# A two-block transformer kernel: other buffers, issue orders and last step in its MLP

## The chip, the cores and the metric

One core of a Trainium2 chip runs the whole program. The metric is the device time of one execution in microseconds, the median of several. Every number below is of this kernel on this chip.

## The reference

Two transformer blocks over 1024 rows of 1024 float32 values; the first (two layers of windowed attention and mLSTM) and the second's mixers are not touched. The change lies in the second block's last lines:

```python
x = x + y @ w_out[l]
xn2 = _rmsnorm(x, norm2_g[l])
x = x + jnp.square(jax.nn.relu(xn2 @ w_up[l])) @ w_down[l]   # 1024 -> 4096 -> 1024
return _rmsnorm(x, final_g)
```

## The kernel before

**Precision.** Float32 factors are split in two parts, a rounded high part (written by ScalarE, `*_hi`) and the rest (`*_lo`, a subtraction by VectorE, DVE, or by GpSimd, POOL). A product is three matmuls: high by high, high by low, low by high. DVE's subtraction is called a split here.

**Seven products.** Both MLP matrices are multiplied by a scheme of seven block products (numbers 1 to 7) in place of eight. Each factor is cut in four blocks; sums of blocks (s1 to s4 of the up weights, t1 to t4 of the down weights, hs1 to hs4 of the hidden part, and row sums of the normed input) are formed by POOL and DVE; the products are added up in seven shared sums.

**Output product and norm** (`output`). TensorE (PE) makes 16 products of 24 matmuls, eight row tiles for each of two column halves. In the second half each tile is added to `x_res` (`residual`), squared (ScalarE), scaled (DVE, `scale_rows`, after POOL's `root`), turned by PE (`turn`, eight transposes), split (`low_rows` for tiles 0 to 3) and, for tiles 4 to 7, made into the row sums that products 5, 6, 7, 3 and 4 need (`rows_low` on DVE: seven instructions; `rows_high` on ScalarE; `low_third` on POOL). The sum for number 4 is made once, by DVE and POOL, and its split is in `up(0)`.

**Up phase** (`up`). Sixteen groups g of 256 hidden units, seven products of 12 matmuls each, in the order `UP_ORDER` = 1, 5, 2, 6, 7, 3, 4. For each group SP's queue loads one 1 MB piece of raw weights (`u_raw`), after all seven splits of the group before; POOL makes s1 to s4 (`sums_up`); ScalarE rounds, DVE splits (`low_up(g + 1, j)`, placed late in `up(g)`), DVE adds PSUM results to h11, u_two, u_four, h22, h21, h12 and squares the four h; POOL makes hs1 to hs4 (`sums_hidden`); SP stores h11, h12, h22 (`store_hidden`) and the sums (`store_sums`) to DRAM. DVE's first addition of a group (h11) waits for the sums and the store of the last group, since they share one buffer.

**Down phase** (`down`). Eight steps w of 512 hidden units, each seven products j of four tiles of 6 matmuls, in the order `DN_ORDER`. SP loads the hidden parts (`load_hidden(w, j)`, each into the slot that product j of the step before frees) and the weights (`load_down`, two halves of `d_raw`). POOL makes t1 to t4 and five of the low parts (`LOW_POOL`); DVE makes the other nine (`LOW_DVE`, by position) and 28 additions. Tile i of the down phase writes bank (i + 4) % 8 and waits until tile i - 8's bank was read (`q_add`); the first eight wait for the up phase's additions. In the last step the shared sums are joined, and then `finish` adds the last four tiles, and each row is squared, scaled and stored from one of two buffers.

**What sets the order.** Each engine runs its instructions in the order of the program; semaphores join them. SP's queue is one such order too: a load behind a wait stands.

## Time and profile before

| | us |
|---|---|
| median of 3 runs | 2792.64 (2783.29 to 2793.39) |
| the profiled execution | 2788.39 |
| its span, first to last instruction | 2786.6 |
| PE busy | 2614.4 (94%) |
| DVE busy | 1758.1 (63%) |
| POOL busy | 861.1 (31%) |
| mean granted TensorE clock | 0.973 |

The profile is of one execution. The changed phases take about its last quarter: output product from 2003, up phase from 2096, down phase from 2437, end at 2786.6. Matmuls are pipelined, so the pitch from start to start tells the pace of PE, and the idle time before an instruction, in brackets, tells what it waited for.

### The profile page before, as it was taken

Reading aid. Unit: us, or ns where it says so; the run is one execution under the profiler, and the core shown is the slowest. Engines: PE = TensorE matmul, PEld = TensorE weight load, DVE = VectorE, ACT = ScalarE, POOL = GpSimd, SP = SyncE. Lnnn points to the kernel's source line nnn. Section 1 sums busy time; section 2 is a strip of 40 time slices with the busy share of each in tenths; the row PEclk is TensorE's granted clock in tenths of the full one; section 3 lists DMA queues with packets and bytes.
Section 4 is the critical chain, followed back from the end, with each engine's and each line's share of the span. In section 5 each row is a group of like instructions: output and inputs, shape, how many; then the busy total and the mean of one; then the engine's idle time right before and its main releaser. Section 6 shows DMA issues by size and latency. Waiting matters only on the chain. (4 is left out here: it accounts for less than half of the span.)

```text
span 2786.6 us, 37933 instructions
## 1 busy us (share of the span) xinstructions
PE 2614.4 (94%) x14936; PEld 2159.8 (78%) x14936; DVE 1758.1 (63%) x2677; ACT 1058.1 (38%) x1999; POOL 861.1 (31%) x582
## 2 busy tenths in 40 slices
PE   6999999999998999999989989999998999889995
PEld 4789888888866798888878768856686877668884
DVE  4312575676544413766765546868648787789998
ACT  3201233666522311335656334278613222233332
POOL 0000100234531001101326400046104656577665
PEclk8999999999999999999999999999999999999998
DMA  7322222136565222321264421100301434454441
GB/s 281 97 87 82 80 76 80 38 92 213 181 233 208 96 77 71 99 80 49 63 216 158 167 98 47 40 16 1 144 1 57 158 134 163 166 184 152 145 159 68
DMA packets 182255, 317.23 MB, mean 114 GB/s; under 512 B 29138, under 2 KB 110724, under 8 KB 174016
## 3 DMA queue, kind: packets, MB, share of 16 engines
q1 hardware_dynamic: 160928, 300.08, 31.9%
q10 hardware_dynamic: 21152, 14.75, 1.7%
q8 instruction: 119, 1.95, 0.3%
q14 instruction: 56, 0.46, 0.1%
HBM read 237.04 MB, written 72.50 MB: 111 GB/s over the span
## 5 line engine op out<-in xcount | busy, mean ns | idle before, releaser
L1026 PE MATMUL ps<-xn_hi_sb,ft_hi_sb 128*128 128x512 f32 (+1 forms) x720 | 264.0, 367 | 1.0 <-DVE ft_lo_sb L1477 1.0
L1027 PE MATMUL ps<-xn_lo_sb,ft_hi_sb 128*128 128x512 f32 (+1 forms) x720 | 263.2, 366 | 0.0
L1028 PE MATMUL ps<-xn_hi_sb,ft_lo_sb 128*128 128x512 f32 (+1 forms) x720 | 262.9, 365 | 0.0
L978 PE MATMUL ps<-tm_hi_sb,xn_hi_sb 128*128 128x512 f32 (+2 forms) x608 | 216.0, 355 | 14.8 <-DVE xn_lo_sb L1391 6.7
L980 PE MATMUL ps<-tm_hi_sb,xn_lo_sb 128*128 128x512 f32 (+2 forms) x608 | 213.3, 351 | 0.0
L979 PE MATMUL ps<-tm_lo_sb,xn_hi_sb 128*128 128x512 f32 (+2 forms) x608 | 213.1, 350 | 0.0
L2285 POOL TENSOR_TENSOR arena_sb<-arena_sb 128x1024 f32<-128x1024 f32 x10 | 25.9, 2591 | 418.7 <-ACT arena_sb L2000 418.7
L1026 PEld LDWEIGHTS ps<-xn_hi_sb,ft_hi_sb 128*128 128x128 f32 x720 | 136.8, 190 | 23.4 <-DVE ft_lo_sb L1477 1.4
L1027 PEld LDWEIGHTS ps<-xn_lo_sb,ft_hi_sb 128*128 128x128 f32 x720 | 136.9, 190 | 21.6
L1028 PEld LDWEIGHTS ps<-xn_hi_sb,ft_lo_sb 128*128 128x128 f32 x720 | 136.8, 190 | 21.7
L2081 ACT ACTIVATE arena_sb<-ps,neg_max_sb 128x640 f32<-128x640 f32 (+1 forms) x144 | 109.3, 759 | 103.7 <-DVE neg_max_sb L1644 97.7
L1643 DVE TENSOR_REDUCE row_max_sb<-ps 128x1 f32<-128x640 f32 (+1 forms) x144 | 111.7, 776 | 46.9 <-PE ps L1073 46.0
L978 PEld LDWEIGHTS ps<-tm_hi_sb,xn_hi_sb 128*128 128x128 f32 x608 | 115.1, 189 | 33.5 <-issue 9.3
L3845 POOL TENSOR_TENSOR arena_sb<-arena_sb 128x512 f32<-128x512 f32 x60 | 75.2, 1274 | 188.0 <-DVE arena_sb L3164 188.0
L2305 POOL CAST q_hl_sb<-arena_sb 64x512 fp32r<-64x512 f32 x36 | 24.2, 671 | 327.9 <-PE ps L1028 289.9
L980 PEld LDWEIGHTS ps<-tm_hi_sb,xn_lo_sb 128*128 128x128 f32 x608 | 115.0, 189 | 11.9
L979 PEld LDWEIGHTS ps<-tm_lo_sb,xn_hi_sb 128*128 128x128 f32 x608 | 115.3, 190 | 10.9
L1083 PE MATMUL ps<-ident_sb,arena_sb 128*128 128x128 f32 x672 | 107.7, 287 | 15.9 <-ACT arena_sb L2081 10.3
L2993 PE MATMUL ps<-xn_hi_sb 128*128 128x512 f32 x256 | 101.2, 395 | 11.2 <-DVE xn_lo_sb L3393 8.2
L2955 PE MATMUL ps<-xn_hi_sb,uq_hi_sb 128*128 128x512 f32 x256 | 102.0, 399 | 10.1 <-DVE uq_lo_sb L3267 6.0
L1226 PE MATMUL ps<-w_out_hi_sb,mix_hi_sb 128*128 128x512 f32 x256 | 105.8, 413 | 4.5 <-DVE mix_lo_sb L1830 4.5
L2272 POOL TENSOR_TENSOR stat_sb<-stat_sb,minus_half_sb 128x1 f32<-128x1 f32 (+1 forms) x48 | 35.7, 743 | 236.2 <-DVE stat_sb L1356 128.4
(491 smaller groups left out, 7505.4 us busy)
## 6 DMA issues: line engine op xcount, KB each, us to landing
arena_sb<-in_w_ft SPq DMA_DIRECT2D x44, 512.0 KB, 3.3
arena_sb<-mqk_dram SPq DMA_DIRECT2D x36, 512.0 KB, 3.7
arena_sb<-x_dram SPq DMA_DIRECT2D x33, 512.0 KB, 7.0
arena_sb<-in_w_ada SPq DMA_DIRECT2D x16, 1024.0 KB, 9.0
u_raw_sb<-in_w_up SPq DMA_DIRECT2D x16, 1024.0 KB, 4.9
hq_dram<-h_part_sb SPq DMA_DIRECT2D x16, 1024.0 KB, 4.1
d_raw_sb<-in_w_down SPq DMA_DIRECT2D x16, 1024.0 KB, 5.6
xn_raw_sb<-hq_dram SPq DMA_DIRECT2D x32, 512.0 KB, 3.6
```

The source lines that it names most:

```text
L978: pe.matmul(at, hi, tm_hi[b][:, k, :], start=k == 0, stop=False)
L979: pe.matmul(at, hi, tm_lo[b][:, k, :], start=False, stop=False)
L980: mm = pe.matmul(at, lo, tm_hi[b][:, k, :], start=False, stop=k == KT - 1)
L1026: pe.matmul(to, hi, xn_hi_flat[:, k, at:at + size], start=k == 0, stop=False)
L1027: pe.matmul(to, hi, xn_lo_flat[:, k, at:at + size], start=False, stop=False)
L1028: mm = pe.matmul(to, lo, xn_hi_flat[:, k, at:at + size], start=False, stop=k == KT - 1)
L1083: mm = pe.transpose(ps[:, bank, at * P:(at + 1) * P], prob[h % 2][:, n * P:(n + 1) * P], ident[:, :])
L1226: pe.matmul(to, hi, w_hi, start=start, stop=False)
L1643: ch(dve, dve.tensor_reduce(row_max[:, u, h:h + 1], at, AX_X, ALU.max, negate=True))
L2081: act.activation(prob[r][:, 0:n], at, ACT.Exp, bias=neg_max[:, u, h:h + 1], scale=DH ** -0.5, accum_out=lsum[:, u, h:h + 1]).then_inc(a_e[ ...
L2955: pe.matmul(to, uq_hi[n][:, k, :], xq_hi[n][:, k, :], start=k == 0, stop=False)
L2993: pe.matmul(to, aq_hi[j][:, k, rows], bq_hi[j][:, k, :], start=k == 0, stop=False)
```

## The change

In the up phase the raw weights get another layout in DRAM. Three of the four blocks stay in one buffer (`u_raw`), the fourth (u22) has two; s3 and s4 get raw buffers of their own. A load waits for the first three splits and the sums of the group before, and for the fourth block for the splits two groups back; it stands ahead of `store_hidden` on SP. DVE's splits are spread over the group, the first at its head. The stored pair is now h11 and h22.

In `output` the row sums of tiles 4 to 7 are two instructions before the scaling of the next tile, one between its mean and its scaling, two behind; ScalarE makes copies for them (`first_high`, and in `rows_high`). The turn of tile 6 comes before the first up product. DVE adds the sum for number 4 instead of POOL.

`DN_ORDER` becomes 1, 2, 6, 5, 3, 7, 4. The splits for down step 0 stand between the additions of up group 15. In steps 0 to 5, DVE makes the splits of positions 5 and 6 ahead of the last four additions. The last step (512 units) is eight plain block products in place of seven: 16 output tiles of 12 matmuls, row by row; groups 14 and 15 need no hidden sums, and POOL makes only two low parts. DVE joins the shared sums for rows 0 to 3, POOL for rows 4 to 7, and each row is squared, scaled and stored as it ends.

```diff
 xq_hi[n], xq_lo[n] = rounded(f"xq{n}_hi", at, 4, HALF), rounded(f"xq{n}_lo", at + 2048, 4, HALF)
...
-u_raw = apart("u_raw", M2, KT, FG)
-u11, u12, u21, u22 = [u_raw[:, 4 * k:4 * k + 4, P * n:P * n + P] for n in range(2) for k in range(2)]
-u_at = [M2 + 2048 + 1024 * j for j in range(6)] + [M2 + 17984]
+u_raw = apart("u_raw", M2, 3, 4, P)
+u11, u12, u21 = [u_raw[:, n] for n in range(3)]
+u22 = [apart(f"u22{i}", at, 4, P) for i, at in enumerate((M2 + 1536, M2 + 16448))]
...
-LOW_DVE = ((0, 0), (0, 1), (2, 0), (2, 1), (3, 1), (1, 1), (4, 1), (5, 1), (6, 1))
-LOW_POOL = (3, 1, 4, 5, 6)
+LAST = WIDE - 1
+LOW_DVE = ((0, 0), (0, 1), (1, 0), (1, 1), (2, 1), (3, 1), (4, 1), (5, 1), (6, 1))
...
+def raw_free(g):
+    if g > 0:
+        sp.wait_ge(u_lo, 7 * g - 4)
+        sp.wait_ge(u_sum, 4 * g)
 def load_up(g):
-    sp.dma_start(u_raw, A["w_up"][g]).then_inc(u_ld, 16)
+    raw_free(g)
+    sp.dma_start(u_raw, A["w_up"][g][:, 0:3]).then_inc(u_ld, 16)
+    if g == 1:
+        sp.wait_ge(norm_sems["2"]["tr"], NX - 1)
+    elif g > 1:
+        sp.wait_ge(u_lo, 7 * g - 7)
+    sp.dma_start(u22[g % 2], A["w_up"][g][:, 3]).then_inc(u_ld, 16)
...
+    sp.wait_ge(u_h, 4 * g + 2)
+    sp.dma_start(hq_dram[g // 2][:, 0:2, g % 2, :], h_part[:, 0:2, :]).then_inc(hq_a, 16)
 def store_sums(g):
+    if g // 2 == LAST:
+        sp.wait_ge(u_h, 4 * g + 4)
+        sp.dma_start(hq_dram[LAST][:, 5:7, g % 2, :], h_part[:, 5:8:2, :]).then_inc(hq_s, 16)
...
-for g in range(GROUPS):
-    if g + 1 < GROUPS:
-        sp.wait_ge(u_lo, 7 * g + 7)
-        load_up(g + 1)
+load_up(1)
+for g in range(GROUPS - 1):
     if g > 0:
         store_sums(g - 1)
-    if g + 1 < GROUPS:
-        store_hidden(g)
-sp.wait_ge(u_lo, 7 * GROUPS)
-load_down(0, 0)
+    if g + 2 < GROUPS:
+        load_up(g + 2)
+    else:
+        raw_free(GROUPS)
+        sp.wait_ge(u_lo, 7 * GROUPS - 7)
+        load_down(0, 0)
+    store_hidden(g)
+store_sums(GROUPS - 2)
 load_hidden(0, 0)
 sp.wait_ge(up_mm, up_no(GROUPS - 1, 5))
 load_down(0, 1)
...
     load_hidden(0, j)
 store_hidden(GROUPS - 1)
+for j in range(5, 7):
+    load_hidden(0, j)
...
-    load_hidden(w, 0)
     sp.wait_ge(t_sum, 4 * w - 1)
     sp.wait_ge(q_lo, 9 * w - 7)
     load_down(w, 0)
+    load_hidden(w, 0)
     sp.wait_ge(t_sum, 4 * w)
-    sp.wait_ge(q_lo, 9 * w - 1)
+    sp.wait_ge(q_lo, 9 * w - 2)
     load_down(w, 1)
-    for j in range(1, 7):
+    for j in range(1, 4 if w == LAST else 7):
...
     pe.wait_ge(norm_sems["2"]["ev_dve"], 4)
     product(0, 1)
-    turn("2", nx_s2, NX - 2, 0)
+    turn("2", nx_s2, NX - 1, 1)
     product(0, 2)
-    turn("2", nx_s2, NX - 1, 1)
...
+    def last_product(t, c):
+        i, row, rows = 28 * LAST + 2 * t + c, t // 4, slice(t % 4 * P, (t % 4 + 1) * P)
+        if t % 4 == 0:
+            pe.wait_ge(q_lo, 9 * LAST + 6)
+            pe.wait_ge(q_lop, 5 * LAST + 2)
+        to = ps[:, (i + 4) % 8, :]
+        pe.wait_ge(q_add, i - 7)
+        for m in range(2):
+            a, b = 2 * row + m, 2 * c + m
+            for k in range(2):
+                pe.matmul(to, aq_hi[a][:, k, rows], bq_hi[b][:, k, :], start=m == 0 and k == 0, stop=False)
+                pe.matmul(to, aq_hi[a][:, k, rows], bq_lo[b][:, k, :], start=False, stop=False)
+                mm = pe.matmul(to, aq_lo[a][:, k, rows], bq_hi[b][:, k, :], start=False, stop=m == 1 and k == 1)
+        mm.then_inc(q_mm2, 1)
+    for w in range(LAST):
...
+    def first_rows(t):
+        t1 = xq_raw[5][:, :, at]
         dve.wait_ge(s["tr"], t + 1)
+        dve.tensor_tensor(t1, top, t1, ALU.subtract).then_inc(t_row, 1)
+        dve.wait_ge(t_high, high_t(n, "x22"))
+        dve.tensor_tensor(xq_lo[3][:, :, at], bottom, xq_hi[3][:, :, at].bitcast(F32), ALU.subtract).then_inc(t_row, 1)
+    def second_rows(t):
+        u, n, at = t % 2, t - 4, slice((t - 4) * P, (t - 3) * P)
+        bottom = ps[:, 2 * u + 1, :].rearrange("p (k q) -> p k q", k=4)
+        dve.wait_ge(t_row, row_no(n, "t1"))
+        dve.tensor_tensor(xq_raw[6][:, :, at], bottom, xq_raw[5][:, :, at], ALU.subtract).then_inc(t_row, 1)
+    def third_rows(t):
+        s, u, n, at = norm_sems["2"], t % 2, t - 4, slice((t - 4) * P, (t - 3) * P)
+        bottom = ps[:, 2 * u + 1, :].rearrange("p (k q) -> p k q", k=4)
+        t3 = xq_raw[7][:, :, at]
         dve.wait_ge(s["ev_act"], t + 1)
+        dve.tensor_tensor(t3, bottom, t3, ALU.subtract).then_inc(s["ev_dve"], 1)
         dve.wait_ge(t_high, high_t(n, "t1"))
+        dve.wait_ge(t_row, row_no(n, "t2"))
+        dve.tensor_tensor(xq_lo[5][:, :, at], xq_raw[5][:, :, at], xq_hi[5][:, :, at].bitcast(F32), ALU.subtract).then_inc(t_low, 1)
...
     dve.wait_ge(g2_ld, 16)
     for t in range(NX):
         residual(1, t)
-        scale_rows("2", x_res[:, t, :], g2_row, nx_s2[t % 2], t)
         if 1 <= t <= 4:
             low_rows("2", xn2_hi, xn2_lo, t - 1)
         elif t > 4:
-            rows_low(t - 1)
-    rows_low(NX - 1)
+            first_rows(t - 1)
+        mean_square("2", t)
+        if t > 4:
+            second_rows(t - 1)
+        scale_row("2", x_res[:, t, :], g2_row, nx_s2[t % 2], t)
+        if t > 4:
...
+        lows(0)
+        dve.wait_ge(hq_a, 16 * g)
+        dve.wait_ge(u_hs, min(4 * g - 1, 4 * (GROUPS - 2)))
     dve.wait_ge(up_mm, up_no(g, 2))
     dve.wait_ge(u_p1, g + 1)
-    if g > 0:
-        dve.wait_ge(hq_a, 16 * g)
-        dve.wait_ge(u_hs, 4 * g)
     dve.tensor_tensor(h11, p1_copy, bank(2), ALU.add).then_inc(u_add, 1)
+    if g == 0:
+        lows(0)
+        dve.wait_ge(t_high, 17)
+        dve.tensor_tensor(xq_lo[4], xq_raw[4], xq_hi[4].bitcast(F32), ALU.subtract).then_inc(t_low, 1)
+    lows(1)
     dve.wait_ge(up_mm, up_no(g, 6))
     dve.tensor_tensor(u_two, p1_copy, bank(6), ALU.add).then_inc(u_add, 1)
     dve.wait_ge(u_add, add_no(g, "c11"))
     squared(h11).then_inc(u_h, 1)
-    if g == 0:
-        dve.wait_ge(t_high, 13)
-        dve.tensor_tensor(xq_lo[4], xq_raw[4], xq_hi[4].bitcast(F32), ALU.subtract).then_inc(t_low, 1)
     dve.wait_ge(up_mm, up_no(g, 5))
     dve.wait_ge(u_add, add_no(g, "u2"))
     dve.tensor_tensor(u_four, u_two, bank(5), ALU.add).then_inc(u_add, 1)
-    if g + 1 < GROUPS:
-        low_up(g + 1, 0)
-        low_up(g + 1, 1)
-        low_up(g + 1, 2)
+    lows(2)
+    next_quads(0, 1)
     dve.wait_ge(up_mm, up_no(g, 7))
     dve.wait_ge(u_add, add_no(g, "u4"))
     dve.tensor_tensor(h22, u_four, bank(7), ALU.add).then_inc(u_add, 1)
     dve.tensor_tensor(u_two, u_two, bank(7), ALU.add).then_inc(u_add, 1)
-    dve.wait_ge(up_mm, up_no(g, 3))
-    dve.tensor_tensor(h21, u_four, bank(3), ALU.add).then_inc(u_add, 1)
+    lows(3)
     dve.wait_ge(u_add, add_no(g, "c22"))
     squared(h22).then_inc(u_h, 1)
+    lows(4)
+    next_quads(2, 3)
+    dve.wait_ge(up_mm, up_no(g, 3))
+    if g == GROUPS - 1:
+        dve.wait_ge(hq_s, 16 * g)
+    dve.tensor_tensor(h21, u_four, bank(3), ALU.add).then_inc(u_add, 1)
     dve.wait_ge(u_add, add_no(g, "c12"))
     squared(h21).then_inc(u_h, 1)
-    if g + 1 < GROUPS:
-        low_up(g + 1, 3)
-        low_up(g + 1, 4)
-    else:
-        for m in range(4):
-            low_quad(0, *LOW_DVE[m])
+    lows(5)
+    next_quads(4, 5)
     dve.wait_ge(up_mm, up_no(g, 4))
     dve.wait_ge(u_add, add_no(g, "u7"))
+    if 0 < g < GROUPS - 1:
+        dve.wait_ge(hq_s, 16 * g)
     dve.tensor_tensor(h12, u_two, bank(4), ALU.add).then_inc(u_add, 1)
     dve.wait_ge(u_add, add_no(g, "c21"))
     squared(h12).then_inc(u_h, 1)
-    if g + 1 < GROUPS:
-        low_up(g + 1, 5)
-        low_up(g + 1, 6)
-    else:
-        for m in range(4, 7):
-            low_quad(0, *LOW_DVE[m])
+    lows(6)
+    next_quads(6)
 def low_quad(w, j, b):
...
+    def lows(*which):
+        for m in which:
+            if w + 1 < LAST or m < 6:
+                low_quad(w + 1, *LOW_DVE[m])
...
-        join(lambda t: sum6[t], sum1)
-    for t in range(4):
...
+def last_down():
...
+    def add(t, c):
+        i = 28 * LAST + 2 * t + c
+        x = x_res[:, t, 512 * c:512 * (c + 1)]
+        dve.wait_ge(q_mm2, i + 1)
+        dve.wait_ge(q_both, 8 + 2 * t + c + 1) if t < 4 else dve.wait_ge(q_join, 4 * (t - 4) + 2 * (c + 1))
+        dve.tensor_tensor(x, x, ps[:, (i + 4) % 8, :], ALU.add).then_inc(q_add, 1)
...
-    pool.tensor_tensor(s1, u21, u22, ALU.add).then_inc(u_sum, 1)
+    pool.tensor_tensor(s1, u21, u22[g % 2], ALU.add).then_inc(u_sum, 1)
+    if g == 1:
+        pool.wait_ge(norm_sems["2"]["tr"], NX)
+    if g > 0:
+        pool.wait_ge(u_lo, 7 * g - 2)
+    pool.tensor_tensor(s3_raw, u11, u21, ALU.subtract).then_inc(u_sum, 1)
     if g > 0:
         pool.wait_ge(up_mm, up_no(g - 1, 6))
     pool.wait_ge(u_sum, 4 * g + 1)
     pool.tensor_tensor(s2, s1, u11, ALU.subtract).then_inc(u_sum, 1)
-    if g > 0:
-        pool.wait_ge(up_mm, up_no(g - 1, 3))
-    pool.wait_ge(u_sum, 4 * g + 2)
-    pool.tensor_tensor(s4, u12, s2, ALU.subtract).then_inc(u_sum, 1)
+        pool.wait_ge(u_lo, 7 * g - 1)
+    pool.wait_ge(u_sum, 4 * g + 3)
...
+    if w == LAST:
+        low_quad(2)
+        low_quad(3)
...
+    low_quad(2)
     low_quad(3)
-    low_quad(1)
-    if w == 0:
-        sums_hidden(GROUPS - 1)
-    slot_free(pool, w, 4)
+    slot_free(pool, w, 5)
     pool.tensor_tensor(t3, b22, b12, ALU.subtract).then_inc(t_sum, 1)
     low_quad(4)
-    low_quad(5)
     slot_free(pool, w, 6)
     pool.wait_ge(t_sum, 4 * w + 2)
     pool.tensor_tensor(t4, b21, t2_raw, ALU.subtract).then_inc(t_sum, 1)
+    low_quad(5)
     low_quad(6)
+def last_joins(t):
+    for c, what in ((0, sum6), (0, sum7), (1, sum5), (1, sum7)):
+        x = x_res[:, 4 + t, 512 * c:512 * (c + 1)]
+        if what is sum7:
+            pool.wait_ge(q_join, 4 * t + 2 * c + 1)
+        pool.tensor_tensor(x, x, what[t], ALU.add).then_inc(q_join, 1)
 sums_up(0)
```

## Rows read from the trace of the kernel before

**Rows 1.** Busy time by stretch; the first line names the columns.
```profile
core 0: us, PE busy (x) PEld busy (x) DVE busy (x) ACT busy (x) POOL busy (x), PEclk, DMA share, GB/s
2096.00:2134.00 38.00, 26.64 (x103) 20.77 (x102) 33.40 (x35) 13.04 (x20) 16.50 (x8) 0.82 0.08 28
2134.00:2429.00 295.00, 288.93 (x1260) 235.19 (x1259) 231.21 (x272) 67.92 (x116) 178.33 (x118) 1.00 0.39 144
2429.00:2463.00 34.00, 16.44 (x54) 12.41 (x53) 19.51 (x17) 12.64 (x13) 26.21 (x12) 0.77 0.73 273
2463.00:2719.00 256.00, 256.00 (x1126) 211.27 (x1125) 253.57 (x250) 96.20 (x96) 176.93 (x62) 1.00 0.45 152
2757.00:2787.00 30.00, 0.20 (x1) 0.00 (x0) 20.78 (x32) 8.97 (x16) 6.91 (x9) 0.57 0.34 140
```
**Rows 2.** Waits, 2134 to 2429 (who <- for whom: total us, times, longest).
```profile
ACT uq_hi_sb L3523 <- DMA u_raw_sb<-in_w_up: 162.9, 14, 11.9
...
DVE h_part_sb L3341 <- POOL h_part_sb L3882: 58.4, 15, 3.9
```
**Rows 3.** Timeline of PE: starts of two up groups, of two down steps.
```profile
2153.12 0.50 PE L2955 MATMUL ps<-xn_hi_sb,uq_hi_sb 128*128 128x512 f32 x1
...
2172.79 0.50 PE L2955 MATMUL ps<-xn_hi_sb,uq_hi_sb 128*128 128x512 f32 x1 [0.34 <-DVE uq_lo_sb L3267]
...
2566.64 0.39 PE L2993 MATMUL ps<-xn_hi_sb 128*128 128x512 f32 x1
...
2604.72 0.39 PE L2993 MATMUL ps<-xn_hi_sb 128*128 128x512 f32 x1
```
**Rows 4.** Up group 0: line L2955 (durations, first and last start), timelines.
```profile
L2955 PE MATMUL ps<-xn_hi_sb,uq_hi_sb x256: 389/389/792, 2096.1 to 2425.8; 128*128 128x512 f32 x128
...
2103.58 2.27 DVE L3040 SCALAR_TENSOR_TENSOR arena_sb<-arena_sb,stat_sb,small_sb 128x1024 f32<-128x1024 f32 x1 [0.66 <-POOL stat_sb L3825]
...
2111.86 0.79 PE L2955 MATMUL ps<-xn_hi_sb,uq_hi_sb 128*128 128x512 f32 x1 [3.98 <-DVE xn_lo_sb L3286]
...
2118.11 6.67 POOL L3929 TENSOR_TENSOR xq_raw_sb<-xq_raw_sb,xn_lo_sb 128x2048 f32<-128x2048 f32 x1
...
2124.81 1.92 ACT L3775 ACTIVATE xq_hi_sb<-xq_raw_sb 128x2048 fp32r<-128x2048 f32 x1 [9.43 <-POOL xq_raw_sb L3929]
...
2129.38 0.50 PE L2955 MATMUL ps<-xq_hi_sb,uq_hi_sb 128*128 128x512 f32 x1 [3.25 <-DVE xq_lo_sb L3348]
...
2133.83 0.39 PE L2955 MATMUL ps<-xn_hi_sb,uq_hi_sb 128*128 128x512 f32 x1
```
**Rows 5.** Timelines of DVE and POOL inside one down step.
```profile
2580.46 1.21 DVE L3393 TENSOR_TENSOR xq_lo_sb<-xq_raw_sb,xq_hi_sb 128x1024 fp32r<-128x1024 f32 x1
...
2594.42 5.76 POOL L3896 TENSOR_TENSOR xq_lo_sb<-xq_raw_sb,xq_hi_sb 128x1024 fp32r<-128x1024 f32 x2
...
2597.86 3.41 DVE L3393 TENSOR_TENSOR xq_lo_sb<-xq_raw_sb,xq_hi_sb 128x1024 fp32r<-128x1024 f32 x1
...
2606.91 2.47 DVE L3409 TENSOR_TENSOR arena_sb<-arena_sb,ps 128x512 f32<-128x512 f32 x4
```
**Rows 6.** Timelines of SP's queue and PE at the hand-over.
```profile
2425.35 0.50 SPq L2612 DMA_DIRECT2D d_raw_sb<-in_w_down  x1
...
2428.98 0.39 PE L2957 MATMUL ps<-xq_hi_sb,uq_lo_sb 128*128 128x512 f32 x1
...
2461.17 0.77 PE L2993 MATMUL ps<-xn_hi_sb 128*128 128x512 f32 x1 [3.04 <-DVE sum_sb L3407]
```
**Rows 7.** Timelines of the last down step and the tail.
```profile
2718.96 0.39 PE L2993 MATMUL ps<-xn_hi_sb 128*128 128x512 f32 x1
...
2756.82 0.39 PE L2995 MATMUL ps<-xq_hi_sb,xq_lo_sb 128*128 128x512 f32 x1
...
2773.80 1.06 ACT L3511 ACTIVATE arena_sb<-arena_sb 128x1024 f32<-128x1024 f32 x1 [0.75 <-DVE stat_sb L3019]
...
2776.06 0.54 POOL L3825 TENSOR_TENSOR stat_sb<-stat_sb,minus_half_sb 128x1 f32<-128x1 f32 x1 [1.76 <-DVE stat_sb L3019]
...
2780.64 1.28 DVE L3326 SCALAR_TENSOR_TENSOR out_s_sb<-arena_sb,stat_sb,final_g_sb 128x1024 f32<-128x1024 f32 x1 [0.56 <-DMA out<-out_s_sb]
```

268 lines of the change are left out of this document (128 added, 140 removed).

## The prediction

> **What bounds the kernel now.** I read the busy time by stage first, then what waited for whom, then the timelines around each gap. TensorE sets the time. From the first product of the up phase to the last of the down phase it issues matmuls back to back except in four places [rows 1]. The pitch: product 0 of one down step starts at 2566.64 and of the next at 2604.72 [rows 3]; 168 matmuls lie between, so 38.08/168 = 0.2267 us each, a product of 12 matmuls takes 2.72 us, and an up group of 84 takes 19.04 us. What is over that is the loss. (a) Up group 0 starts at 2096.1, group 1 at 2133.83 [rows 4]: 37.7 where 19.0 would do, loss 18.7. (b) Groups 1 to 15 end at 2429.2 (last matmul plus one pitch [rows 6]): 295.4 where 15 x 19.04 = 285.6 would do, loss 9.8; in the row of one boundary the groups start 19.67 apart [rows 3]. (c) The third product of the down phase starts at 2461.17, where 2429.2 + 4 x 2.72 = 2440.1 was possible, and its first matmuls still last 0.77 [rows 6]: loss 21 and about 1.5 of slow clock, 22.5. (d) After the last matmul (2756.82) comes a tail up to 2786.6: 29.8 [rows 7].
>
> Two waits explain (b): the loads of raw weights, on which ScalarE waits 162.9 us in all, and DVE's first addition of a group, which waits 58.4 us for POOL's sums of the hidden part [rows 2]. The splits then come in a burst and the next group's first one is late.
>
> **Part 1, raw weights in two buffers, loads first in SP's order.** The load of group g+2 now goes when the third split of g+1 and POOL's four sums are done, and the first split of the next group stands at the head of DVE's group. I walked one group (its first product starts at 0). POOL's s2 waits for the product of number 6 (10.9) and ends near 12.4 (1.2, half of POOL's 2.3 at 1024 wide [rows 5]). DVE's operations from there are short: 0.6 each for additions out of PSUM (2.47 for four [rows 5]) and, at half the width of the 1.21 split, 0.6 for a split or a square; twelve or so bring it to 23. DVE next has to be at h11 at 8.5 of the following group, which is 27.5. The store of h11 goes at 19.1 behind the load on SP and has 8 us to land; the load goes at 16.8 and is needed at 22. All have over 3 us to spare, so (b) goes: -9.5. What is late next is nothing within 3 us. Behind the new wait of SP (third split of g+1) stands the store of h11, and behind that DVE's h11; if the cover of 4 us were gone, each microsecond would cost 15.
>
> **Part 2, row norm interleaved.** The row sums of one tile go from seven DVE instructions to five, and the scaled row stands between them, not before them. Before, DVE delayed the scaled row of the last tile to 2103.58 and product three of group 0 to 2111.86 [rows 4]. In the new order DVE's tile costs seven operations of 0.6 or so (additions out of PSUM, below), the scaling at 1.2 (1.28 with its overlap [rows 7]), in all near 5 us, under TensorE's 24 matmuls and one turn a tile (24 x 0.2267 = 5.4 and the turn); 1.1 more where POOL's third split collides with the scaling (2.27 instead of 1.28 [rows 4, 7]). I get: scaled row 6 at 2096.3, scaled row 7 at 2103.8, the turn until 2104.8, product three at 2104.9. So 7 us earlier; but TensorE still idles 3.6 before that turn, and runs slow again for some 2 us, as after the gap of 3.25, where 12 matmuls took 2133.83 - 2129.38 = 4.45 instead of 2.72 [rows 4]. The sum for number 4 leaves POOL (6.67 beside DVE [rows 4]) for DVE (2.3). It is followed by ScalarE's rounding (1.92 [rows 4]), a first split of group 1 that waits for its rounding, and the 2048-wide split (2.3, twice the 1.13 of a 1024-wide one): ready near 2123, while TensorE asks at 2120.5; with the product and a slow start group 1 begins at 2127.3. Gain 6.5; 5 to 9 are open.
>
> **Part 3, hand-over to the down phase.** Before, the down weights went out at 2425.35, behind the store of the sums [rows 6], and groups 14 and 15 had sums to store. Now d_raw's first half goes in group 14, hidden part 0 goes at 4 us of group 15, and DVE's splits stand between its additions. With free engines product 0 would be ready at 15, before TensorE asks (19.05), and (c) would vanish. But POOL's 2.3 us operations and DVE's with two SBUF inputs do not overlap: alone DVE's split takes 1.21, beside POOL 3.41, and POOL's pair takes 5.76 [rows 5]. The order is strictly alternating in these rows: 3.41 is POOL's 2.3 and then DVE's 1.1. In group 15 POOL has nine such operations from 11.2 on (product 6 frees t1's slot) and DVE seven splits and four squares, each of which waits for one of POOL's. Step by step: t1 to 13.4, square 14.0, t2 16.3, split 17.4, POOL 19.7, split 20.8: product 0 starts at 21 (late 2.0). Then POOL 23.1, square 23.7, POOL 26, split 27.1, POOL 29.4, split 30.5: product 1 starts at 30.6 instead of 26.4 (4.2). Then h21, square behind POOL 33.4, split 36.8, split 40.2, and h12 only at 40.8: the eighth down tile needs the bank that h12 reads and stands from 34.8 to 40.9 (6.1, in which the slow clock after the earlier gap is hidden); 0.6 more for the ninth tile, and 1.5 of slow clock. Loss 14.4 instead of 22.5: gain 8. Ends: nothing gained, if loads land 8 us late as several did in 2429 to 2463 (DMA share 0.73 [rows 1]); 22.5 if POOL's operations come in other gaps.
>
> The Trainium skill (SBUF — State Buffer, section Who interferes with whom) says that a DVE instruction with two SBUF inputs and a GpSimd instruction that reads SBUF exclude each other for their whole length, and that the issue order decides who waits. The rows at 3.41 against 1.21 agree; if they shared bandwidth evenly instead, the alternation above would not hold and this part would be worth more.
>
> **Part 4, down steps.** Products have another order, and DVE now makes two splits (positions 5 and 6 of LOW_DVE) ahead of the last four additions of a step instead of one. In the profile these additions begin at 2606.91 [rows 5]; one more split beside POOL is +3.40, the first addition ends at 2610.31 + 0.60 = 2610.9. The bank it frees is wanted by tile 5 of the next step at 2604.72 + 5.44 = 2610.16. So TensorE waits 0.8 in each of six steps: +5 (0 to 8; at 0 if POOL's ops end a little earlier). The clock stays high over such gaps, as over the 0.34 at a group boundary [rows 3]; I take that to hold for 0.8 too.
>
> **Part 5, the last 512 units by plain products.** 16 tiles of 12 matmuls instead of 168: +24 x 0.2267 = +5.4. Against it the tail shrinks, since tiles finish row by row. Before, from the first matmul of the last step (2718.96) to the end is 67.7 [rows 7]. After: TensorE ends at 43.5. DVE's 16 joins start at 1 and collide with POOL's four to a row; DVE is at its first addition at 15.8, loses 1.1 to POOL's joins at each scaling, and waits for root 3, which stands behind POOL's fourth row of joins (37.5). It catches up at 2.5 us a row: additions of row 7 at 45.0, square 1.25 and root 0.54 [rows 7], last scaling ends at 48.3. From the last scaling's end (2780.64 + 1.28) to the end of the span were 4.7, so 53.0. Gain 14.7, against 17 if DVE were never late and 10 if POOL's joins cost 5 us more.
>
> **Sum.** 9.5 + 6.5 + 8 - 5 + 14.5 = 33.5. The profiled execution took 2788.4 (span 2786.6), so 2755; it lies 4.2 under the median of the runs shown (2792.6), and against that median the sum gives 2759. I take 2758, since the runs spread over 10 us.
>
> **Rivals.** *A: the hand-over and the down steps keep TensorE fed* (POOL's operations fall beside additions out of PSUM, which don't collide). For: in the profile 256 us of the down phase pass without a gap though DVE is shown busy all the time [rows 1]. Against: the alternation in [rows 5]. Gain 9.5 + 6.5 + 22 + 0 + 14.5 = 52: 2740. *B: the hand-over only moves its wait and the last step is bound by POOL's 16 joins*: 9.5 + 4 + 0 - 7 + 9 = 15: 2777. *C, slower: the chain SP to DVE in the up phase.* The store of h11 stands on SP behind a load that waits for the third split of the next group, h11 of the next group waits for that store, and the splits come behind h11. If that ring takes longer than a group's 19.04, every group is late. It has about 4 us of slack by my walk; it decides from there, and to eat 48 us (33.5 and 14 more) it has to run at 22.3 a group: 2807. Against it: DVE is busy 231 of 295 [rows 1] and POOL 178, waiting for each other included. *D: the change doesn't remove the boundary waits* (a split of the next group is still last): 24 of gain, 2769, inside my range.
>
> **How the numbers follow.** Chances: forecast with its neighbours (D too) 0.68, A 0.15, B 0.11, C 0.06. Range 2742 to 2775: it takes in the bounds of part 3 and part 4 up to nearly A and nearly B. A measurement of this kernel can tell about 0.5% (14 us) from no change. B is half under that, so faster 0.87, same 0.08, slower 0.05.
>
> **What would show it.** Up groups 19.05 apart with no gap before their first matmul (part 1); product three of group 0 near 2105 and group 1 near 2127; down product 1 waiting for DVE's split and the eighth down tile waiting for h12 (part 3); gaps of 0.8 before the fifth tile of each down step, released by DVE's addition (part 4); a tail after the last matmul near 9.5 us instead of 29.8. Wrong would be: groups over 19.5 apart, or a hand-over with loads as its last wait.

## The result, and the profile after

| | before | changed |
|---|---|---|
| median, us | 2788.62 (4 runs, 2783.29 to 2793.39) | 2757.02 (4 runs, 2754.36 to 2764.34) |
| the profiled execution | 2788.39 | 2755.82 |
| its span | 2786.6 | 2754.1 |
| mean granted TensorE clock | 0.973 | 0.979 |

The ratio is 0.9891 with a 95% interval of 0.9861 to 0.9921: 1.1% faster. The forecast was 2758, from 2742 to 2775. The median before now has a fourth run in it (2784.6); the prediction reckoned from 2792.64, the median of the first three.

First the windows of the changed kernel's profile, cut at its own stage bounds, in answer to [rows 1] (time, then busy us and count for PE, weight loads, DVE, ACT and POOL, granted clock, DMA share, GB/s):

```profile
2097.00:2126.00 29.00, 22.53 (x97) 17.94 (x96) 25.90 (x26) 13.24 (x21) 12.34 (x8) 0.94 0.03 10
2126.00:2413.00 287.00, 287.00 (x1261) 236.36 (x1259) 214.45 (x270) 75.75 (x122) 177.06 (x115) 1.00 0.45 162
2413.00:2437.00 24.00, 14.72 (x50) 10.73 (x49) 23.93 (x15) 6.46 (x7) 19.70 (x7) 0.83 0.23 81
2437.00:2700.00 263.00, 258.66 (x1130) 212.28 (x1130) 252.48 (x256) 92.34 (x92) 161.06 (x56) 1.00 0.46 151
2743.00:2754.00 11.00, 0.56 (x3) 0.13 (x1) 5.59 (x8) 2.30 (x4) 1.55 (x3) 0.65 0.47 191
```

PE is now busy for all of the 287 us of groups 1 to 15. What is left lies in up group 0 (22.5 busy of 29), in the hand-over (14.7 of 24) and, new, in the down steps: 258.7 of 263, where the kernel before was busy for all of 256. To put numbers on it I take from the timelines the start of each stage's first matmul, and call "loss" what a stage takes over its matmuls times 0.2267 us.

| stage | before | changed | difference | forecast |
|---|---|---|---|---|
| start of the execution to the output product | 2003.25 | 2002.02 | -1.2 (same code) | 0 |
| output product to group 1's start | 130.58 | 123.99 | -6.6 | -6.5 |
| groups 1 to 15, loss | 9.78 | 1.60 | -8.2 | -9.5 |
| end of up phase to down product 2, loss | 21.09 | 13.08 | -8.0 | -8 |
| product 2 to the last step, loss | 2.07 | 6.99 | +4.9 | +5 |
| last step and tail | 67.65 | 54.18 | -13.5 | -14.5 |
| sum | | | -32.6 | -33.5 |

Two rows of this table share a boundary that the forecast drew elsewhere. In the kernel before, 1.6 us of slow matmuls follow the start of down product 2 (granted clock 0.50 from 2461.2 to 2464.0), in the changed kernel 1.0; the forecast counted them in the hand-over, the table in the row below. By the forecast's cut the hand-over gained 8.6 (for 8) and the down steps cost 5.5 (for 5).

The loads no longer stand in the way. Waits between 2126 and 2413, in answer to [rows 2] (who waits for whom: total us, times, longest); 162.9 us of waiting have become 3.2:

```profile
DVE h_part_sb L3411 <- PE ps L2983: 20.2, 12, 4.8
...
ACT uq_hi_sb L3578 <- DMA u_sb<-in_w_up: 3.2, 4, 1.4
```

PE's timeline, in answer to [rows 3] (start, duration, engine, line, operation; in brackets idle time before it and what ended it). Two groups start 19.14 apart with no bracket, two down steps 39.09 apart where it was 38.08, and inside the step stands a wait for DVE's addition:

```profile
2126.01 0.39 PE L2981 MATMUL ps<-xn_hi_sb,uq_hi_sb 128*128 128x512 f32 x1
...
2145.15 0.39 PE L2981 MATMUL ps<-xn_hi_sb,uq_hi_sb 128*128 128x512 f32 x1
...
2465.35 0.39 PE L3018 MATMUL ps<-xn_hi_sb 128*128 128x512 f32 x1
...
2471.68 0.47 PE L3018 MATMUL ps<-xq_hi_sb 128*128 128x512 f32 x1 [0.73 <-DVE arena_sb L3479]
...
2504.44 0.39 PE L3018 MATMUL ps<-xn_hi_sb 128*128 128x512 f32 x1
```

Group 0, all engines, in answer to [rows 4]. The last scaling now ends at 2103.57, product number 2 of the group starts behind the turn at 2104.48, and product number 4 waits for its split (L3415):

```profile
2101.29 2.28 DVE L3087 SCALAR_TENSOR_TENSOR arena_sb<-arena_sb,stat_sb,small_sb 128x1024 f32<-128x1024 f32 x1
...
2103.63 1.09 PE L2693 MATMUL ps<-ident_sb,arena_sb 128*128 128x128 f32 x8 [3.33 <-DVE arena_sb L3087]
2104.48 0.60 PE L2981 MATMUL ps<-xn_hi_sb,uq_hi_sb 128*128 128x512 f32 x1
...
2118.07 1.71 DVE L3314 TENSOR_TENSOR uq_lo_sb<-u_raw_sb,uq_hi_sb 128x512 fp32r<-128x512 f32 x1 [1.91 <-ACT uq_hi_sb L3578]
2119.70 3.35 DVE L3415 TENSOR_TENSOR xq_lo_sb<-xq_raw_sb,xq_hi_sb 128x2048 fp32r<-128x2048 f32 x1
...
2123.11 0.50 PE L2981 MATMUL ps<-xq_hi_sb,uq_hi_sb 128*128 128x512 f32 x1 [3.13 <-DVE xq_lo_sb L3415]
```

The hand-over, in answer to [rows 6]. The down weights go out at 2391.01, 22 us ahead of the end of the up phase, where it was 4 (2425.35 and 2429.2). PE now waits three times, always for DVE, and of DVE's seven splits there five take 3.4 us (the first 2.85; the last, with GpSimd done, 1.22). DVE has no idle time between 2405.2 and 2436, so it wasn't waiting for a load or for ScalarE:

```profile
2391.01 0.35 SPq L2634 DMA_DIRECT2D d_raw_sb<-in_w_down  x1
...
2411.51 3.43 DVE L3465 TENSOR_TENSOR xn_lo_sb<-d_raw_sb,xn_hi_sb 128x1024 fp32r<-128x1024 f32 x1
2414.99 0.50 PE L3018 MATMUL ps<-xn_hi_sb 128*128 128x512 f32 x1 [1.63 <-DVE xn_lo_sb L3465]
...
2419.97 3.33 POOL L3965 TENSOR_TENSOR xn_lo_sb<-xn_raw_sb,xn_hi_sb 128x1024 fp32r<-128x1024 f32 x1
2421.02 3.36 DVE L3465 TENSOR_TENSOR xq_lo_sb<-d_raw_sb,xq_hi_sb 128x1024 fp32r<-128x1024 f32 x1
...
2424.43 0.50 PE L3018 MATMUL ps<-xq_hi_sb 128*128 128x512 f32 x1 [3.67 <-DVE xq_lo_sb L3465]
...
2433.71 0.68 DVE L3447 TENSOR_TENSOR h_part_sb<-u_two_sb,ps 128x512 f32<-128x512 f32 x1
2434.44 0.79 PE L3018 MATMUL ps<-xq_hi_sb 128*128 128x512 f32 x1 [3.98 <-DVE h_part_sb L3447]
```

The tail, in answer to [rows 7]. PE ends at 2743.17, the last scaling starts 4.9 us later, where it was 23.8:

```profile
2743.17 0.39 PE L3035 MATMUL ps<-xq_hi_sb,xq_lo_sb 128*128 128x512 f32 x1
...
2748.10 1.28 DVE L3385 SCALAR_TENSOR_TENSOR out_s_sb<-arena_sb,stat_sb,final_g_sb 128x1024 f32<-128x1024 f32 x1 [0.66 <-POOL stat_sb L3891]
```

### The profile page after: what moved, and what is told of

Same layout as the page of the kernel before. It is cut to its first block and busy times, and to the rows that moved or that the text cites. A ratio compares the mean times of both kernels' runs of the same rounds, so it can differ in the third digit from the quotient of the medians.

```text
span 2754.1 us, 37985 instructions
## 1 busy us (share of the span) xinstructions
PE 2615.1 (95%) x14960; PEld 2162.6 (79%) x14960; DVE 1722.1 (63%) x2651; ACT 1055.9 (38%) x2001; POOL 826.5 (30%) x570
## 5 line engine op out<-in xcount | busy, mean ns | idle before, releaser
L1034 PEld LDWEIGHTS ps<-xn_hi_sb,ft_lo_sb 128*128 128x128 f32 x720 | 136.5, 190 | 21.6
L1234 PE MATMUL ps<-w_out_hi_sb,mix_lo_sb 128*128 128x512 f32 x256 | 104.0, 406 | 0.0
L1233 PE MATMUL ps<-w_out_lo_sb,mix_hi_sb 128*128 128x512 f32 x256 | 103.4, 404 | 0.0
```

Source lines behind the costliest of these rows:

```text
L1034: mm = pe.matmul(to, lo, xn_hi_flat[:, k, at:at + size], start=False, stop=k == KT - 1)
```

## The experiments

All are edits of the changed kernel and were profiled once; in most the reading is by stage, not by the whole time. There is a reason. The same kernel, profiled twice (all3 and all3_timed, below), took 724.45 and 724.47 us from the start of the output product to its end, but 1997.55 and 2010.79 before that, in code that no experiment touches. So a stage tells more than the whole, which moves by 13. How well it repeats depends on the stage: over the runs that leave them alone, the loss of groups 1 to 15 was 1.6 to 1.7 us, of the hand-over 12.9 to 13.1, from product 2 to the last step 6.3 to 7.4. Group 0 is the exception, see experiment 3.

**1. The hand-over: DVE against GpSimd, or the transfers?** Two runs. In the first GpSimd (POOL) pauses:

```diff
                     low_quad(3)
+                    if w == 0:
+                        pool.wait_ge(u_h, 4 * GROUPS)
                     slot_free(pool, w, 5)
```

> Edit: in the first down step GpSimd waits, before its third sum and the four operations behind it, until VectorE has squared the last part of h. Alternation theory: the hand-over's 13 us of loss come from VectorE's splits and squares taking turns with GpSimd's operations (3.4 us instead of 1.2), so with GpSimd quiet from about 2417 on the two gaps before product 1 and tile 8 (4.05 and 4.38 us) shrink below 1 us, the two of product 0 stay (2.0), the loss of the hand-over falls from 13.1 to 2.5 to 4 and the span by 9 to 11 us. Rival, the transfers of the down weights and of h set the hand-over: the gaps stay within 0.5 us, or GpSimd's delay makes the splits of operands 4 to 6 late and product 4 or later waits several us.

Measured: 2749.21. The hand-over's loss fell from 13.1 to 2.7, as the alternation theory said, but the span fell by only 6.7, not by 9 to 11 (1.4 of it ahead of the output product): behind product 2 the loss rose from 7.0 to 12.1. That is the rival's second half in size, several us at a later product, though not its cause: PE waits for a bank that DVE's copies free, not for a late split. The timelines of this run show the price:

```profile
2440.89 3.13 POOL L3980 TENSOR_TENSOR t_raw_sb<-d_raw_sb,xq_raw_sb 128x1024 f32<-128x1024 f32 x1 [0.17 <-POOL xq_raw_sb L3973]
2441.73 3.38 DVE L3465 TENSOR_TENSOR xn_lo_sb<-d_raw_sb,xn_hi_sb 128x1024 fp32r<-128x1024 f32 x1
2445.03 2.47 DVE L3477 COPY h_part_sb<-ps 128x512 f32<-128x512 f32 x4
2445.86 0.76 PE L3018 MATMUL ps<-xn_hi_sb 128*128 128x512 f32 x1 [3.29 <-DVE h_part_sb L3477]
```

GpSimd's put-off work meets the splits for the next step at 2441, the copies behind them come late, and PE waits for a bank.

In the second run GpSimd writes zeros in the first step and reads nothing; its four sums of the down weights (t1 shown) and its five low parts become:

```diff
+                        if w == 0:
+                            pool.memset(to, 0.0).then_inc(t_sum, 1)
+                        else:
+                            pool.tensor_tensor(to, a, b, ALU.subtract).then_inc(t_sum, 1)
...
-                    pool.tensor_tensor(t1, b12, b11, ALU.subtract).then_inc(t_sum, 1)
+                    difference(t1, b12, b11)
...
+                        if w == 0:
+                            pool.memset(aq_lo[j].bitcast(F32), 0.0).then_inc(q_lop, 1)
+                            return
```

> In the first down step GpSimd writes zeros instead of its four sums and five low parts (their values are left out), so it reads nothing while VectorE works. Alternation theory: VectorE's splits take 1.2 us and its squares 1.1 each, all three gaps of the hand-over go, its loss falls from 13.1 to 0.5 to 2.5 us and the span by 10.5 to 12.5. Rival, the loads of weights and h or ScalarE's copies set it: loss stays at 11 to 13 us. Third case, part of it is VectorE's own order of work: 3 to 8 us stay.

Measured: 2736.66, hand-over loss 0.03 us, less than any of the three cases gave. Nothing of the 13 us was the loads', ScalarE's or DVE's own. The zeros also take less time than the sums (0.95 us for 2.4), so this run alone doesn't part GpSimd's reads from its lateness; the run handover below does, since GpSimd does all its work there and the loss is 0.03 too. DVE's splits in this run:

```profile
2407.21 1.22 DVE L3465 TENSOR_TENSOR xq_lo_sb<-d_raw_sb,xq_hi_sb 128x1024 fp32r<-128x1024 f32 x1
...
2413.26 1.22 DVE L3465 TENSOR_TENSOR xn_lo_sb<-d_raw_sb,xn_hi_sb 128x1024 fp32r<-128x1024 f32 x1
```

while GpSimd's zeros were written in the same microseconds:

```profile
2407.38 0.95 POOL L3972 MEMSET xq_lo_sb<- 128x1024 f32 x1 [0.94 <-ACT xq_hi_sb L3853]
...
2414.27 0.95 POOL L3972 MEMSET xq_lo_sb<- 128x1024 f32 x1 [0.94 <-ACT xq_hi_sb L3853]
```

A GpSimd operation that only writes costs DVE nothing. The Trainium skill says so too (SBUF — State Buffer, section Who interferes with whom: a DVE instruction with two SBUF inputs contends with a GpSimd instruction that reads SBUF, "not with one that only writes it"); this trace agrees, with 1.22 beside the zeros and 3.4 beside the sums.

**2. The gaps of the down steps.**

```diff
-                    lows(5, 6)
+                    lows(5)
                     adds(6)
+                    lows(6)
```

> Edit: in each down step the second of the two splits ahead of the last four additions goes behind them. My theory, that the two splits hold back the additions that free the banks: the six gaps of 1.1 us before tile 5 of steps 1 to 6 vanish, a step takes 38.1 instead of 39.1 us, the span falls by 5 to 6 us. Rival, ScalarE's high parts or GpSimd's low parts of the next step are late there: the steps stay at 39.0 to 39.1. Price to be seen: if the moved split is itself late, a new gap before product 4 of each step (the split is needed about 20 us later, so none expected).

Measured: 2752.0. The steps are 38.08 apart, the six gaps are gone, the loss from product 2 to the last step is 0.88 instead of 6.99: 6.1 us, by one split that is moved behind four additions. No new gap appeared. The theory holds.

**3. What won group 0: the new order of the row work, or the earlier turn?**

```diff
+                    product(0, 2)
                     turn("2", nx_s2, NX - 1, 1)
-                    product(0, 2)
```

> Edit: the turn of the last row tile stands behind the second product of group 0 again instead of ahead of it. My theory, that group 1's start is set by the chain from the last scaling over sums and the fourth operand's split and not by the place of the turn: the turn starts at the same time after the last output product within 0.3 us, the idle of 3.3 us ahead of it becomes work, the gap ahead of group 0's last product grows from 3.5 to about 6, and group 1 starts at the same time within 0.5 us; span unchanged within 1 us. Rival, the earlier turn is what won time in group 0: group 1 starts 2.5 to 3 us later.

Measured: 2764.09, of which 5.3 us lie ahead of the output product; group 0 loses 12.2 instead of 9.7, so group 1 comes 2.5 us later, which is the rival's figure. But product 4 does start at the same time after the group's first product (25.94 us, against 25.82), as my theory said. PE had waited 4.0 us for it instead of 3.1 (I had expected 2.5 more; waits of 1.4 and 1.6 ahead of products 3 and 6 took the rest). PE's timeline of this run, and the window of product 4:

```profile
2128.56 0.79 PE L2981 MATMUL ps<-xq_hi_sb,uq_hi_sb 128*128 128x512 f32 x1 [4.00 <-DVE xq_lo_sb L3415]
```

```profile
2128.60:2133.80 5.20, 5.20 (x12) 4.08 (x13) 5.20 (x9) 0.00 (x0) 0.00 (x0) 0.50 0.27 73
```

The granted clock over product 4 is 0.50, that is the level of 1.2 GHz, and its 12 matmuls are 0.43 apart instead of 0.23: 2.4 us. In the changed kernel the same product ran at 1.00 (2.4 GHz), and it was product 2, behind the 3.3 us wait ahead of the turn, that ran slow: its 12 matmuls took 4.4 us instead of 2.7, at no cost to group 1, since product 4 waits for DVE in any case. Two windows of the changed kernel, the first with product 2 and the start of product 3, the second with product 4:

```profile
2104.00:2110.00 6.00, 6.00 (x24) 4.86 (x23) 6.00 (x8) 3.97 (x7) 3.26 (x2) 0.72 0.00 0
...
2123.10:2126.00 2.90, 2.89 (x12) 2.37 (x13) 2.90 (x6) 0.00 (x0) 0.00 (x0) 1.00 0.02 6
```

Is the slow product 4 the turn's doing? Another run says that it need not be. load_late (experiment 4) has the changed kernel's order in group 0, the turn early, and PE's timeline there is that of the changed kernel up to product 4, with a wait of 3.17 us before it; yet that product ran at 0.50 and group 0 lost 12.1 us. PE's timeline and the window of product 4 in load_late:

```profile
2133.53 0.79 PE L2981 MATMUL ps<-xq_hi_sb,uq_hi_sb 128*128 128x512 f32 x1 [3.17 <-DVE xq_lo_sb L3415]
```

```profile
2133.50:2138.80 5.30, 5.27 (x12) 4.13 (x13) 5.30 (x10) 0.00 (x0) 0.00 (x0) 0.50 0.02 3
```

Of the six runs with this order (the changed kernel, pool_waits, pool_blank, split_behind, handover and load_late), whose waits there are 3.13 to 3.36 us, five went on at 1.00 and this one at 0.50. So the 2.4 us can fall on either place of the turn, and with one run of turn_late it isn't shown that the early turn wins anything. What won group 0 is then the new order of the row work and of the sum for number 4, by elimination and not by a run of its own.

**4. Part 1, taken apart.** The change made the load early and spread the splits. Three runs: the load late again (load_late, in `raw_free`), the splits bunched again (splits_bunched), both (late_bunched).

```diff
-                        sp.wait_ge(u_lo, 7 * g - 4)
+                        sp.wait_ge(u_lo, 7 * g)
```

The bunched splits, 0 to 2 behind u_four, 3 and 4 behind the third square, 5 and 6 behind the last; the first of the three places:

```diff
-                        lows(0)
...
-                    lows(1)
...
-                    lows(2)
+                    lows(0, 1, 2)
                     next_quads(0, 1)
```

> Edit: the load of a group's three raw quarters waits again until all seven splits of the group before are done, as in the kernel before; the spread places of the splits and the second buffer of the fourth quarter stay. Theory: either half of part 1 alone takes up the boundary's slack, so groups 1 to 15 lose 1.6 to 4 us in all (1.6 now, 9.8 before). Rival L, the early load is what removed the loss: 8 to 12 us. Rival S, only the places of the splits count: 1.6 as now.

> Edit: the seven splits of the next group stand at their old places in VectorE's order (three after the fourth sum, two after the third square, two after the last), the early load and the two buffers stay. Theory (either half suffices): groups 1 to 15 lose 1.6 to 4 us. Rival L (the load counts): 1.6 as now. Rival S (the places count): 8 to 12 us. For the start of the first group the first split moves behind the fourth operand's, so group 1 may start up to 2 us earlier or, where its first two products then wait for their splits, up to 3 us later.

> Both edits together, which is nearly the order of the kernel before for groups 1 to 15. All theories: the loss of 8 to 12 us is back, span 2761 to 2766 us against the 2754 of the changed kernel; a loss under 5 would say that something else in part 1 (the second buffer, the new places of the sums) removed it.

| | loss of group 0 | loss of groups 1 to 15 | whole time |
|---|---|---|---|
| changed kernel | 9.7 | 1.60 | 2757.02 (median) |
| splits_bunched | 7.3 | 1.70 | 2763.35 (10.5 of it ahead of the output product) |
| load_late | 12.1 | 38.6 | 2812.67 |
| late_bunched | 7.3 | 70.2 | 2835.21 |

My theory that either half is enough has fallen. With the early load the loss is gone wherever the splits stand; with the late load the spread places make it smaller (38.6 against 70.2) and don't remove it. But no statement had the size: rival L gave 8 to 12 us for load_late, and all of them 8 to 12 for late_bunched, so the late load costs far more here than the 9.8 us of the kernel before. In group 0 the bunched places are better: product 4's split no longer stands behind group 1's first, PE waits 0.2 us for it instead of 3.1, and group 1 starts 2.4 us earlier. (load_late's 12.1 is the slow product 4 of experiment 3.) The waits of load_late from 2180 to 2300, and its timelines at one boundary:

```profile
ACT uq_hi_sb L3578 <- DMA u_sb<-in_w_up: 72.0, 5, 14.6
...
DVE uq_lo_sb L3314 <- ACT uq_hi_sb L3578: 33.6, 5, 6.9
```

```profile
2187.80 1.78 DVE L3314 TENSOR_TENSOR uq_lo_sb<-u_sb,uq_hi_sb 128x512 fp32r<-128x512 f32 x1
...
2189.61 0.35 SPq L2607 DMA_DIRECT2D u_raw_sb<-in_w_up  x1
...
2195.63 0.64 ACT L3578 ACTIVATE uq_hi_sb<-u_raw_sb 128x512 fp32r<-128x512 f32 x1 [14.40 <-DMA u_sb<-in_w_up]
2196.30 1.15 DVE L3314 TENSOR_TENSOR uq_lo_sb<-u_raw_sb,uq_hi_sb 128x512 fp32r<-128x512 f32 x1 [6.72 <-ACT uq_hi_sb L3578]
```

Last split ends, load goes (0.03 us later), load lands (6.0), first split of the next group. The first split now stands at the head of DVE's group, so DVE stands 6.7 us with all its work behind it. In late_bunched the first split is behind u_four, but another queue was blocked (waits from 2180 to 2305):

```profile
DVE h_part_sb L3410 <- DMA hq_dram<-h_part_sb: 37.2, 5, 7.6
```

SyncE's order has the store of h behind the load that now waits; DVE's first sum of the next group waits for that store, 7.4 us in each group. This is the ring of rival C, slower than a group: 285.6 + 70.2 over 15 is 23.7 us a group. (In load_late DVE waited for the store once in five groups, 0.9 us; its ring runs from the load over the first split.) To see how much of it is the store, one more run puts it ahead of the load:

```diff
+                    store_hidden(g)
                     if g + 2 < GROUPS:
                         load_up(g + 2)
...
-                    store_hidden(g)
```

> As late_bunched (late load and bunched splits), but SyncE issues the store of h11 and h22 ahead of the late load instead of behind it. In late_bunched VectorE waited 7.4 us in each group for that store (first sum of h, 37 us in the five groups from 2180 to 2305). Theory Q (the late load cost 70 us there only because the store queued behind it): the loss of groups 1 to 15 falls to 8 to 14 us, as the kernel before. Rival (the late load alone costs it): over 30 us stay.

Measured: 2816.51, groups 1 to 15 lose 57.5. The store was 12.7 of the 70.2; theory Q has fallen, though what is left isn't the late load alone either, since the kernel before loads as late and loses 9.8. The timelines of late_bunched2 show where its ring is longer:

```profile
2185.02 0.34 SPq L2607 DMA_DIRECT2D u_raw_sb<-in_w_up  x1
...
2192.09 1.13 DVE L3314 TENSOR_TENSOR uq_lo_sb<-u_raw_sb,uq_hi_sb 128x512 fp32r<-128x512 f32 x1 [4.70 <-ACT uq_hi_sb L3573]
2195.62 0.69 DVE L3314 TENSOR_TENSOR uq_lo_sb<-uq_raw_sb,uq_hi_sb 128x512 fp32r<-128x512 f32 x1 [2.40 <-POOL uq_raw_sb L3930]
...
2208.55 0.35 SPq L2607 DMA_DIRECT2D u_raw_sb<-in_w_up  x1
```

From load to load it is 23.5 us. The second split waits 2.4 us for GpSimd's third sum, where the kernel before needed only its second, and the two loads of a group land 6.4 us after the first one's issue (2191.4, ScalarE's first rounding), where the one load took 5.0. The new order of the sums and the split load are paid for only because the load is early; part 1's edits are not independent of each other. Between this ring and one of the kernel before (loads at 2203.61 and 2223.45, 19.8 apart) lie 3.7 us, and the rows give them as 1.4 for the loads, 2.4 for the third sum, 1.6 for longer work of DVE from the second split to the last, less 1.7 that the first split follows its rounding sooner. That is one group of each; over all groups the difference is 3.2 a group, 47.7 us in all, and no run takes these terms apart. Not all of PE's loss in the late runs is waiting: outside the gaps its matmuls cost 14 us more than in the changed kernel in load_late and 18 in late_bunched and late_bunched2, with a mean granted clock over groups 1 to 15 of 0.97, 0.93 and 0.95 instead of 1.00.

**5. The hand-over again, with DVE's order changed too.** DVE's splits at positions 0 and 1 of `LOW_DVE` go ahead of u_two, those from 5 on into down step 0, one or two between additions; GpSimd's pause comes one operation earlier than in pool_waits, and each step ends as in split_behind.

```diff
+                    next_quads(0, 1)
                     dve.wait_ge(up_mm, up_no(g, 6))
...
-                    next_quads(4, 5)
+                    next_quads(4)
...
                     low_quad(2)
+                    if w == 0:
+                        pool.wait_ge(u_h, 4 * GROUPS)
                     low_quad(3)
```

> Composite from the two runs on the hand-over: VectorE's first two splits of the down part stand ahead of its second sum, its splits of operands 3 to 6 move into the first down step one at a time between additions, GpSimd pauses after three operations until the last square is done, and in every step one split goes behind the last additions. Alternation theory: what counts is how many of VectorE's reads meet GpSimd's before the first bank is copied (about 4 us may be lost there); so the hand-over to product 2 loses 0 to 1.5 us instead of 13.1, and the stretch from there to the last step 1 to 4 instead of 7.0; span lower by 14 to 18 us. Rival, GpSimd's work that was put off meets VectorE later, as in the run with the pause alone (12.1 lost behind product 2): 7 to 12 us stay there and the span falls by only 6 to 10.

Measured: 2754.12 with 10.1 us more ahead of the output product. The hand-over loses 0.03; from product 2 to the last step it is 8.2, inside the rival's bounds: waits of 3.0 us ahead of the second step and 3.3 ahead of its product 1, the second followed by slow matmuls. The steps behind it run at 38.08. From the output product to the end it is 11.8 us less than the changed kernel, under the 14 to 18 of the theory and over the 6 to 10 of the rival.

**6. Everything together.** all2 takes this hand-over, with DVE's splits 5 and 6 back at their places and GpSimd's third sum first after the pause, and adds new orders in the output pass and in group 0. In the output pass the scaling goes ahead of the low parts of the tile before (for tiles 5 to 7 ahead of `xq_lo[3]` too), and GpSimd's low parts wait for the last two scalings. In group 0 the last sum for number 4 goes ahead of number 6's split, products 7 and 6 are exchanged, and number 4's split goes ahead of group 1's first.

```diff
-                        if 1 <= t <= 4:
-                            low_rows("2", xn2_hi, xn2_lo, t - 1)
...
                         scale_row("2", x_res[:, t, :], g2_row, nx_s2[t % 2], t)
+                        if 1 <= t <= 4:
+                            low_rows("2", xn2_hi, xn2_lo, t - 1)
...
                     if t >= 6:
+                        pool.wait_ge(norm_sems["2"]["xs"], t + 1)
                         low_third(t - 6)
```

> Composite. Output pass and group 0: the scaling of a row tile ahead of the low parts of the tile before it, GpSimd's low parts behind the last two scalings, the fourth operand's last sum ahead of the sixth operand's split and products six and seven exchanged, fourth operand's split ahead of group 1's first. Hand-over: first two splits ahead of the second sum, GpSimd pauses after three operations until the last square and then makes its third sum first. Steps: one split behind the last additions. Theory: output pass minus 1.3 us, group 0 loses 3 to 5.5 instead of 9.7, hand-over 0 to 1 instead of 13.1, from there to the last step 0.9 to 3 instead of 7.0; in all 20 to 26 us less than the changed kernel from the start of the output pass on. Rival for the steps: GpSimd's work that was put off meets the first step's splits, and 6 to 9 us stay there, as in the run handover (8.2).

Measured: 2744.36 (7.2 us more ahead of the output product). Output product to the end of its last matmul: 92.65 instead of 94.16; group 0 loses 4.8, hand-over 0.03, and the rival is right for the steps: 7.75. From the output product to the end that is 18.6 us less, short of the 20 to 26 expected. PE waited for DVE's copies behind two contended splits (3.39 and 3.40; the second shown):

```profile
2439.49 3.40 DVE L3472 TENSOR_TENSOR xn_lo_sb<-d_raw_sb,xn_hi_sb 128x1024 fp32r<-128x1024 f32 x1
2442.81 2.47 DVE L3484 COPY h_part_sb<-ps 128x512 f32<-128x512 f32 x4
...
2443.63 0.47 PE L3018 MATMUL ps<-xn_hi_sb 128*128 128x512 f32 x1 [2.35 <-DVE h_part_sb L3484]
```

In all3 ScalarE takes the eight copies of products 3 and 5 of step 0 from DVE, GpSimd starts the second step's t1 only after DVE's first two splits for that step, and in group 0 it starts group 1's s1 only after number 4's split. The edit also moves splits of DVE within step 0, which the expectation doesn't name: positions 2 and 3 behind the fifth product's additions, 5 behind the last ones. What each edit is worth was not taken apart.

```diff
+                def first_sums(j, sums):
...
+                    for t in range(4):
+                        act.wait_ge(q_mm2, 4 * j + t + 1)
+                        act.activation(sums[t], ps[:, (4 * j + t + 4) % 8, :], ACT.Copy).then_inc(q_add, 1)
...
+                    if w == 1:
+                        pool.wait_ge(q_lo, 11)
...
+                    if g == 1:
+                        pool.wait_ge(t_low, 6)
```

> As all2, with three edits more. In the first down step ScalarE copies the sums of the fourth and sixth product out of PSUM instead of VectorE; GpSimd starts the second step's sums only after VectorE's first two splits for it; and in group 0 GpSimd's sums for group 1 wait until the fourth operand is split. Theory (in all2 VectorE's queue in the first step was 2.7 and 3.7 us late because 3.4 us splits and additions fill it): 4.8 us of work less on VectorE and three or four splits at 1.2 instead of 3.4 us bring the loss from product 2 to the last step from 7.7 to 0 to 2.5 us; group 0 loses 3 to 4 instead of 4.8; together the stretch from the start of the output pass to the end is 6 to 9 us shorter than in all2. Rival: GpSimd's or ScalarE's put-off work comes late in the second step, 4 us or more stay there.

Measured: 2724.22. From the start of the output product to the end 724.45 us, against 752.04 for the changed kernel: 27.6 less, and 9.0 less than all2's 733.40. The windows of all3 show PE busy in every microsecond from the hand-over to the last step:

```profile
2091.00:2113.00 22.00, 20.75 (x96) 16.23 (x94) 19.09 (x19) 10.15 (x17) 8.67 (x6) 1.00 0.04 12
2113.00:2401.00 288.00, 287.68 (x1263) 236.64 (x1262) 219.10 (x278) 76.98 (x126) 180.68 (x118) 1.00 0.45 162
2401.00:2439.00 38.00, 38.00 (x169) 31.46 (x168) 32.15 (x32) 19.14 (x24) 26.46 (x11) 1.00 0.59 199
2439.00:2667.00 228.00, 228.00 (x1008) 188.79 (x1007) 224.13 (x227) 83.80 (x84) 153.81 (x53) 1.00 0.46 148
```

Group 0 loses 3.2, groups 1 to 15 2.2 (0.6 more, nearly all in group 1, where PE waits for an addition of DVE), the rest nothing. The same kernel, timed:

> The kernel of all3 again, timed in five rounds against the kernel before. The change itself gave a ratio of 0.989; by stages all3 is 30.8 us shorter than the changed kernel from the start of the output pass to the end (724.5 us against 752.0 would be 27.6; the rest of a difference of single runs lies ahead of the output pass, which is the same code and varied from 1997 to 2014 us in the runs so far). Expected ratio 0.977 to 0.981, time 2724 to 2738 us. If it came out at 0.985 or more, gaps closed in one profiled execution would not be what the mean execution gains.

Measured: 2734.42 (median of 5), ratio to the kernel before 0.9793, interval 0.9779 to 0.9807. It beats both; the change itself stands at 0.9891. (The 30.8 us in the expectation is a slip of mine; its own figures, 752.0 less 724.5, give 27.5.)

## Why the prediction was right

The total was right to 1 us, and, what counts more, nearly so by its steps; but one reason was wrong, one cost was missed, and part of the agreement is luck. The 2758 was reckoned from a median of 2792.6; with the fourth run that is 2788.6, so the gain between medians is 31.6 us, against 33.5 by the sum, and the profiled executions differ by 32.6. Part 2's errors cancel; parts 1 and 5 fell short by 2.3 together, and 1.2 of that came back ahead of the output product, in code that the change doesn't touch.

**Part 1** (forecast -9.5, measured -8.2). The boundary waits went, as walked. The 1.6 us that are left are no gap. Groups start 19.14 apart where 84 matmuls take 19.04; the pitch is 0.231 to 0.236 in product number 4 and in the group's first matmuls. Why was not tried; number 4's weights are the ones that the change moved to another place in SBUF. That spreading the splits matters as much as the load was not in the sum, but it was my theory in experiment 4, and it fell: all of the gain hangs on the early load. The ring of rival C, to which I gave 0.06, is real. It shows once the load waits for all seven splits and stands ahead of the store: 23.7 us a group in late_bunched, where 22.3 was the pace that I gave it, and 12.7 us of the loss went with the store moved ahead. The larger part, in load_late (21.6 a group) too, is a ring without the store, from the load over the splits to the next load. In the changed kernel neither ring decides.

**Part 2** (-6.5, measured -6.6). The scaled row of the last tile was forecast to end at 2103.8 and ended at 2103.57; but the output product started 1.2 us earlier in this execution, and counted from its start the row came 1.0 us late (101.55 for 100.55). Group 1 was forecast 124.05 us after that start and came after 123.99. Two things cancel. The output pass grew by 1.5 us (92.62 to 94.16 us to its last matmul), since the scaling there now stands behind the low parts of the tile before. That is the missed cost; all2, with the scaling first, got it back (92.65). And of the two slow starts in my walk the first came (1.7 us for the 2 forecast, behind the wait ahead of the turn; it costs nothing, as product 4 waits for DVE), while the second, 1.6 us at product 4, did not: granted clock 1.00. That is luck of the execution. In load_late the same order met it, and group 1 came after 126.44.

**Part 3** (-8, measured -8.0). The walk with strict alternation gave 2.0, 4.2 and 6.1 us for three waits. The rows of after show product 0 late by 1.8 (2413.20 to 2414.99), product 1 by 4.0, and the eighth tile by 5.9 in all: 1.8 of slow clock, which I had counted as hidden in the wait, and a wait of 4.15 by the pitch. The 0.6 for the ninth tile did not come, and 1.4 of slow clock stands for the 1.5. The run without GpSimd's reads left 0.03 us, and so did handover, with all of GpSimd's work at other times, so the cause is shown: the exclusion of the two engines, with the slow clock behind the waits that it makes, accounts for all of it.

**Part 4** (+5, measured +4.9). The forecast of 0.8 per step was 0.88, with 0.13 of pitch behind it, so the six gaps cost 6.1 and not 5, and moving one split gave 6.1 back. The 4.9 comes out smaller because the kernel before had slow matmuls of its own in this stretch, 1.6 us behind product 2 (the changed kernel 1.0) and 0.5 later.

**Part 5** (-14.5, measured -13.5). TensorE's part was right (43.3 for 43.5); the last scaling ended 49.5 us after the step's start, not 48.3. The mis-sized term is DVE's catching up after GpSimd's joins. Root 3 came at 2737.68, 37.8 us into the step (forecast 37.5), but from there the rows follow each other at 2.61 us instead of 2.5, so that row 7's second addition started at 2745.35, 45.5 into the step and not 45.0; and from that start to the end of the last scaling it took 4.0 us instead of 3.3, since row 6's scaling stands between.

## What to carry to other kernels

Count the pairs of operations on VectorE and GpSimd that both read SBUF (VectorE with two SBUF inputs) on the path to each bank or operand that TensorE wants: each such pair cost VectorE up to GpSimd's whole operation (3.4 us for 1.2, where GpSimd's alone takes 2.4). Put GpSimd's reads beside additions out of PSUM, let ScalarE take copies where it idles, and read again what GpSimd's put-off work meets next; in three runs here (pool_waits, handover, all2) a part of the wait only moved. When a load is made early, see which queue its wait stands on and what is behind it, and when a product is moved into a gap, see where the idle time goes, since the product behind it may run at half the clock, and in one run but not in the next.

## What was not expected of the hardware

Gaps of nearly the same length ended differently, in the same code. In group 0 of the changed kernel PE idled 3.13 us before product 4, after 15 us of matmuls of which the first 4.4 were slow, and went on at 1.00. In load_late, with the same order and the same matmuls ahead, it idled 3.17 and went on at 0.50; in split_behind it idled 3.36 and went on at 1.00. In pool_waits it idled 3.29 before product 5 of step 0, after 17 us with no gap over 1 us, and the next 12 matmuls came 0.43 apart; in turn_late it idled 4.00, and 12 came so, at 0.50. Each slow start was about 2.4 us more. What decides was not tried, so a single run can't tell an edit that costs 2.4 us here from one that doesn't.

A scaling of 1024 columns by DVE (two inputs in SBUF, L3087 and L3385) takes 1.28 us alone and 2.21 to 2.31 beside a GpSimd operation of 1.3 us: exclusion holds for it as for the splits. In all3 that pair was taken apart at the last scalings, and they took 1.27.
